# Asking for one ScalarE table set, by name, where exponentials and logarithms alternate

## The chip, the core and the metric

The kernel runs on one core of a Trainium2 chip. The metric is the device time of one execution in microseconds (us). Engines: PE is TensorE's matrix multiply and PEld its weight load, DVE is VectorE, ACT is ScalarE, POOL is GpSimd, SP is SyncE, which here only issues DMAs.

## What is computed

Three transformer blocks are applied to x (1 x 512 x 1024, float32), each once. "norm" is `x * rsqrt(mean(x*x) + 1e-6) * g`.

```python
def first_block(x, p, ...):
    h = rmsnorm(x, norm_mix_g)
    mq, mk, mv, mo, mi, mf, dq, dk, dv, gates = split(h @ w_in)
    ...
    logf = log_sigmoid(f_pre)                        # mLSTM, 4 heads
    hd = diff_attention(...); hd = head_rmsnorm(hd)  # softmax(1) - lam * softmax(2)
    x = x + (sigmoid(g_a) * ya + sigmoid(g_b) * yb) @ w_out
    u = causal_dwconv(rmsnorm(x) @ w_up); val, gt = split(u)
    x = x + (gelu(gt) * val) @ w_down
    x = x + sigmoid(rmsnorm(x) @ w_ple_gate) * (p @ w_ple)
    return rmsnorm(x, norm_final_g)
def second_block(x, ...):                            # two layers
    # stick breaking, 16 heads of 64, blocks of 128 queries
    log_fail = where(mask, log_sigmoid(-z), 0); later = reverse cumsum(log_fail) - log_fail
    a = where(mask, exp(log_sigmoid(z) + later), 0);  x = x + ((a @ v) * silu(gate)) @ w_out
    # latent attention, 8 heads: q, k from ranks 256 and 128, normed per head and rotated
    x = x + (causal_softmax_attention(q, k, v) * silu(gate)) @ w_out
def third_block(x, c, ...):                          # shift, scale, gate = silu(c) @ w_ada + b_ada
    x = x + 0.5 * (1 + gate0) * norm(swiglu(modulate(norm(x))))
    x = x + (1 + gate1) * norm(hybrid_mixer(modulate(norm(x))))   # gated unit + forgetting attention
    x = x + 0.5 * (1 + gate2) * norm(swiglu(modulate(norm(x))))
```

## The kernel before

Every engine runs a list of its own, written out in Python; they meet only at semaphores. Activations are kept feature-major: 8 tiles of 128 features by 512 positions. Weights are used once, in panels of 128 x 2048 float32 (1 MB). A panel goes SP DMA, then an ACT cast to the high half WH (`high`, L1110), then four POOL subtractions for the low half WL (L286), then PE. Each product takes three PE passes: high by high, low by high, high by low (L332, L335, L338; in the stretches where PE multiplies eight fresh feature tiles as they come, L432, L433, L435). Almost all of PE's list is such products. DVE adds results to x, makes low halves and does the attention arithmetic between matmuls.

Two kinds of norm exist. `raw` (L1150) gives PE the tiles scaled by the gain alone, the squares are summed on PE beside the work, and the root is applied to the results. `normalise` (L1184) waits for the root and divides first. In both, ACT makes the root (`root`, L1172) as exp(-0.5 ln(mean + eps)): an ACTIVATE with Ln, a drain, an ACTIVATE with Exp. `post_root` (L1156) is the same for the norm behind each of the third block's sub-layers, `mla_root` (L1641) the same for a head of latent attention. The other users of both functions: the log-sigmoid of the mLSTM gates (from L1250), the roots of differential attention (`da_root`, L1330), the ones of the latents, stick breaking (`ln(1 + exp)`, from L1572, 8 pairs of heads, then exp of the strip sums), the forgetting attention's gates, and the pair of norms behind the gated embedding (`raw_final`, L1517, and the roots behind it).

ACT holds one table set at a time. Nobody asks for one in this kernel: the compiler puts an `ACT_TABLE_LOAD` ahead of an ACTIVATE whose function the set at hand lacks. It takes Exp and Ln from two different sets, so that each change between them is a load; Silu, Sigmoid, Gelu and Sqrt have sets of their own. `ln_ahead` (L1169) is a 128 x 1 Ln, run for nothing but the load that it brings ahead of a `root`.

Of ACT's list for an FFN (`ffn`, L1433): it casts panels, makes the root, applies Gelu or Silu to the gate results, and at its end scales and squares tiles for the next norm. Of a pair of stick breaking: two Exp, two Ln, two casts LBH (L1579), a panel cast, a copy, two Exp of the strips. Of a head of latent attention: copies of transposed blocks (L1683), exps of score blocks with a row sum, projections of the head after next, and after block 0 the root of the next head. What PE waits for in such a head is L898 on it, a product with a diagonal matrix that DVE builds (L2409) from that root.

Of the kernel before, what the change touches and what calls it, by code (L numbers as in the profile page):

```python
# [92 lines left out]
def build(nc, x_in, p_in, par_in, con_in, hot_in, rows_in, sguw_in, w_in, ada_in, rel_tmp, out, stage):  # L93
    with ExitStack() as ctx:
# [1004 lines left out]
        def _(act):  # L1099
# [69 lines left out]
            def ln_ahead():  # L1169
                f(COLS[:, 31:32], par("eps"), ACT.Ln)  # L1170
# [32 lines left out]
            def out_gemm(g0, gain, ahead=False):  # L1203
                for q in range(4):
                    if not (ahead and q == 0):
                        next_panel(g0 + q)
                    if not (ahead and q == 1):
                        skip(2)
                    if q:
                        raw(gain, 2 * q - 2, 2 * q)  # L1210
                ln_ahead()
                raw(gain, 6)
                settle()
# [12 lines left out]

            act.wait_ge(sem("par_dma"), 16)
            ln_ahead()
# [21 lines left out]
            act.dma_start(HOT[0:33, 0:NREL], hot_in).then_inc(sem("hot_dma"), 16)  # L1250
            f(LROW[4][0:4, :], LROW[4][0:4, :], ACT.Exp, scale=-1.0)
# [65 lines left out]
            for half in range(2):  # L1317
                vd_copy(1, half)
            act.wait_ge(sem("lams_ready"), 1)
# [109 lines left out]
            ln_ahead()  # L1429
# [3 lines left out]
            def ffn(g0, conv, shift=None, opened=False):  # L1433
# [33 lines left out]
                root()  # L1467
                if not conv:
                    gate(0)
# [19 lines left out]
                if conv:  # L1489
                    for k in range(DT):  # L1490
                        raw(lambda k: par("norm_ple", k), k, k + 1)
                        if k >= 5:
                            embed(k - 5)
                else:
                    ln_ahead()
                    squares(ACC)
# [29 lines left out]
            for k in range(DT):  # L1526
# [7 lines left out]
                if k:  # L1534
                    raw_final(k - 1)
            raw_final(DT - 1)
# [21 lines left out]
            for q in (2, 3):  # L1558
                gate_panel(G_SBG + q, [SG[:, 2 * q, :], SG[:, 2 * q + 1, :]], ACT.Silu)
            for q in range(4):  # L1560
# [51 lines left out]
            mla_gate(0)  # L1612
            b = take()
# [43 lines left out]

            next_panel(mlh(0))
# [48 lines left out]
            act.dma_start(SGW, sguw_in).then_inc(sem("rows_dma"), 16)  # L1707
            act.wait_ge(sem("fz_ready"), 1)
# [12 lines left out]
            act.drain().then_inc(sem("ug_ready"), 1)  # L1721
            act.wait_ge(sem("lv_ready"), 1)
# [74 lines left out]
            ln_ahead()  # L1797
# [1026 lines left out]
```

## Time and profile before

| | |
|---|---|
| time, median of 3 runs | 2598.78 us (2594.71 to 2599.59) |
| time of the profiled execution | 2599.46 us |
| its span | 2597.6 us (1.9 us lie outside) |
| granted TensorE clock, mean | 0.981 of full speed |
| DMA | 245.50 MB, mean 95 GB/s |
| busy | PE 95%, PEld 76%, DVE 49%, ACT 41%, POOL 39% |
| chain that ended last | PE 62%, issue 15%, DVE 8%, POOL 6%, ACT 5% |
| ... of it, line L1104 of ACT | 3% with a tile, 1% without one |

L1104 is the helper through which nearly every ACTIVATE goes. The loads of table sets carry its line too but have no tile, so the last line's 1% is theirs. Matmul records overlap each other; idle time of PE is read from its waits. PEclk is the granted TensorE clock, of which the records show two levels, 1.2 and 2.4 GHz (0.5 and 1.0).

### The profile page before, as it was taken

To read this page: it belongs to the slowest core of one execution; us is meant where nothing else is said; L and a number is where in the kernel's file an instruction comes from. 1 tells how busy PE (TensorE), PEld (TensorE's weight loads), DVE (VectorE), ACT (ScalarE), POOL (GpSimd) and SP (SyncE) were. 2 spreads that over 40 slices of the span, in tenths; PEclk is the share of its full clock that TensorE was granted. 3 is DMA by queue.
4 is the path that set the end of the run, shared out by engine and by line. 5 is a ranking of instruction groups with operands and counts; after the bars stand their busy time and mean duration, and the time that the engine had idled before them with its cause. 6 is when DMAs were issued, how large, how long until landed. Compare 5 with 4: busy or idle time off the path is not lost.

```text
span 2597.6 us, 31125 instructions
## 1 busy us (share of the span) xinstructions
PE 2457.4 (95%) x11642; PEld 1966.0 (76%) x11642; DVE 1274.6 (49%) x1834; ACT 1062.9 (41%) x1377; POOL 1015.7 (39%) x758
## 2 busy tenths in 40 slices
PE   7999999899999989999988899999999998999999
PEld 5887777788887768777766678888868666788886
DVE  5455567866667661444346562222264444422224
ACT  5435775522222543665546542222253434322222
POOL 3332244444444443212443144444434213344442
PEclk9999999999999999999999999999999999999999
DMA  3221596222222222101221122222212101122221
GB/s 139 77 71 66 194 350 257 106 97 97 97 97 86 78 81 81 49 33 49 97 98 55 44 82 97 97 97 97 97 65 94 57 33 65 51 96 97 96 97 65
DMA packets 35956, 245.50 MB, mean 95 GB/s; under 512 B 3951, under 2 KB 4079, under 8 KB 7188
## 3 DMA queue, kind: packets, MB, share of 16 engines
q1 hardware_dynamic: 30096, 207.12, 22.4%
q10 hardware_dynamic: 5764, 37.06, 3.8%
q8 instruction: 65, 1.06, 0.2%
q14 instruction: 31, 0.25, 0.0%
HBM read 242.06 MB, written 2.11 MB: 94 GB/s over the span
## 4 chain that ended last, share of the span: by engine, by line
PE 62%; issue 15%; DVE 8%; POOL 6%; ACT 5%; DVEq 2%; ACTq 0%; POOLq 0%
PE PS L332 17%; PE PS L338 17%; PE PS L335 16%; POOL WL L286 6%; ACT ARENA L1104 3%; PE PS L432 1%; PE PS L435 1%; PE PS L433 1%; ACT L1104 1%; PE PS L821 1%; DVE LBL L2358 1%; PE PS L1018 1%; PE PS L1030 1%; PE PS L792 1%; PE PS L836 1%
## 5 line engine op out<-in xcount | busy, mean ns | idle before, releaser
L286 POOL TENSOR_TENSOR WL<-WT,WH 128x512 fp32r<-128x512 f32 x754 | 1015.5, 1379 | 1549.3 <-ACT WH L1110 1031.3
L332 PE MATMUL PS<-HH,WH 128*128 128x512 f32 x1568 | 623.2, 397 | 32.0 <-DVE ARENA L1910 7.8
L338 PE MATMUL PS<-HH,WL 128*128 128x512 f32 x1568 | 616.3, 393 | 0.0
L335 PE MATMUL PS<-HL,WH 128*128 128x512 f32 x1568 | 615.6, 393 | 0.0
L1452 ACT CAST WH<-WT 128x2048 fp32r<-128x2048 f32 x90 | 172.1, 1912 | 603.3 <-PE PS L332 603.3
L332 PEld LDWEIGHTS PS<-HH,WH 128*128 128x128 f32 x1568 | 297.8, 190 | 108.6 <-issue 19.5
L338 PEld LDWEIGHTS PS<-HH,WL 128*128 128x128 f32 x1568 | 297.4, 190 | 63.4
L335 PEld LDWEIGHTS PS<-HL,WH 128*128 128x128 f32 x1568 | 297.8, 190 | 60.0 <-issue 0.5
L332 PE MATMUL PS<-YH,WH 128*128 128x512 f32 x840 | 331.2, 394 | 8.0 <-ACT ARENA L1104 3.6
L338 PE MATMUL PS<-YH,WL 128*128 128x512 f32 x840 | 327.3, 390 | 0.0
L335 PE MATMUL PS<-YL,WH 128*128 128x512 f32 x840 | 327.1, 389 | 0.0
L1104 ACT ACTIVATE ARENA<-PS 128x512 f32<-128x512 f32 (+1 forms) x159 | 108.8, 691 | 320.6 <-PE PS L338 220.5
L1110 ACT CAST WH<-WT 128x2048 fp32r<-128x2048 f32 (+1 forms) x99 | 187.6, 1895 | 122.7 <-PE PS L332 100.0
L1104 ACT ACTIVATE ARENA<-ARENA 128x512 f32<-128x512 f32 (+5 forms) x225 | 181.0, 817 | 95.4 <-DVEq L1870 25.5
L2200 DVE TENSOR_TENSOR ARENA<-PS,ARENA 128x512 f32<-128x512 f32 x44 | 30.4, 692 | 376.0 <-PE PS L338 376.0
L332 PEld LDWEIGHTS PS<-YH,WH 128*128 128x128 f32 x840 | 157.7, 188 | 49.3 <-ACT ARENA L1104 5.5
L338 PEld LDWEIGHTS PS<-YH,WL 128*128 128x128 f32 x840 | 157.7, 188 | 33.5 <-POOL WL L286 0.2
L335 PEld LDWEIGHTS PS<-YL,WH 128*128 128x128 f32 x840 | 157.8, 188 | 31.5 <-issue 0.2
L2228 DVE TENSOR_TENSOR ARENA<-PS,ARENA 128x512 f32<-128x512 f32 x176 | 121.3, 691 | 106.3 <-PE PS L338 104.4
L1104 ACT ACT_TABLE_LOAD x103 | 132.1, 1283 | 13.5 <-DVE ARENA L1914 7.2
L432 PE MATMUL PS<-HH,WH 128*128 128x512 f32 x240 | 103.2, 430 | 23.4 <-DVE HL L1841 22.4
L332 PE MATMUL PS<-WH,HH 128*128 128x256 f32 x384 | 111.6, 291 | 7.2 <-DVE HL L1863 5.2
(296 smaller groups left out, 3220.9 us busy)
## 6 DMA issues: line engine op xcount, KB each, us to landing
WT<-weights SPq DMA_DIRECT2D x188, 1024.0 KB, 4.9
ARENA<-w_ada ACTq DMA_DIRECT2D x33, 1024.0 KB, 7.1
ARENA<-w_ada SPq DMA_DIRECT2D x3, 1024.0 KB, 7.6
X<-x_fm SPq DMA_DIRECT2D x4, 512.0 KB, 8.0
out_fm<-X SPq DMA_DIRECT2D x8, 256.0 KB, 2.1
ARENA<-rel_rows ACTq DMA_DIRECT2D x1, 1024.0 KB, 5.3
CON<-constants SPq DMA_DIRECT2D x1, 640.0 KB, 11.5
WT<-weights SPq DMA_DIRECT2D x1, 512.0 KB, 5.0
```

The source lines that it names most:

```text
L286: i = nc.gpsimd.tensor_tensor(WL[s][:, e], WT[s][:, e], WH[s][:, e].bitcast(F32), ALU.subtract)
L332: i0 = nc.tensor.matmul(o, w[0], r[0], start=first, stop=False, skip_group_check=True)
L335: nc.tensor.matmul(o, w[0], r[1], start=False, stop=False, skip_group_check=True)
L338: i2 = nc.tensor.matmul(o, w[1], r[0], start=False, stop=last, skip_group_check=True)
L432: i0 = nc.tensor.matmul(psb(b), w[0], src[0][:, k, :], start=k == 0, stop=False, skip_group_check=True)
L433: i1 = nc.tensor.matmul(psb(b), w[0], src[1][:, k, :], start=False, stop=False, skip_group_check=True)
L435: i2 = nc.tensor.matmul(psb(b), w[1], src[0][:, k, :], start=False, stop=k == DT - 1, skip_group_check=True)
L1104: return nc.scalar.activation(o, i, fn, **kw)
L1110: nc.scalar.copy(WH[s][:, 0:width], WT[s][:, 0:width]).then_inc(sem("w_hi"), 1)
L1452: nc.scalar.copy(WH[s][:, :], WT[s][:, :]).then_inc(sem("w_hi"), 1)
L2200: free(tt(GT[:, q, :], psb(b), GE[:, q, :], ALU.mult), b)
L2228: tt(dst[:, j, :], psb(4 + j % 4), dst[:, j, :], ALU.add).then_inc(sem("b_read"), 1)
```

## The change

All of it is on ACT. `ln_ahead` becomes `ln_exp_table`, which emits one load of the set `natural_log_exp_and_others` by name. It holds both functions. It stands where `ln_ahead` stood and at nine more places in the code, ahead of each stretch that uses Exp and Ln. Inside such a stretch the compiler then adds no load of its own. In `ffn` the set of Gelu or Silu is asked for right behind the root. Nothing is computed differently apart from the tables that Exp and Ln are read from.

```diff
--- before.py
+++ after.py
@@ -1166,8 +1166,8 @@
                     f(SQP[:, k, :], X[:, k, :], ACT.Square).then_inc(sem("sq_ready"), 1)
                 settle(acc=0)
 
-            def ln_ahead():
-                f(COLS[:, 31:32], par("eps"), ACT.Ln)
+            def ln_exp_table():
+                nc.scalar.preload_act_table_set("natural_log_exp_and_others")
 
             def root():
                 act.wait_ge(sem("ms_ready"), n["ms"])
@@ -1208,7 +1208,7 @@
                         skip(2)
                     if q:
                         raw(gain, 2 * q - 2, 2 * q)
-                ln_ahead()
+                ln_exp_table()
                 raw(gain, 6)
                 settle()
 
@@ -1224,8 +1224,8 @@
                     b = take()
                     free(f(dst[q], psb(b), fn), b)
 
+            ln_exp_table()
             act.wait_ge(sem("par_dma"), 16)
-            ln_ahead()
             high(0, 0, PANEL // 2)
             for k in range(DT):
                 if k == 6:
@@ -1248,6 +1248,7 @@
             normalise(last=2, meanwhile=og_last)
             act.wait_ge(sem("az_ready"), 1)
             act.dma_start(HOT[0:33, 0:NREL], hot_in).then_inc(sem("hot_dma"), 16)
+            ln_exp_table()
             f(LROW[4][0:4, :], LROW[4][0:4, :], ACT.Exp, scale=-1.0)
             act.drain()
             f(LROW[4][0:4, :], LROW[4][0:4, :], ACT.Ln, bias=1.0).then_inc(sem("lf_ready"), 1)
@@ -1316,6 +1317,7 @@
             f(MCOL[:, 3, :], MCOL[:, 3, :], ACT.Sqrt, scale=1.0 / P).then_inc(sem("mrs_ready"), 1)
             for half in range(2):
                 vd_copy(1, half)
+            ln_exp_table()
             act.wait_ge(sem("lams_ready"), 1)
             f(COLS[:, 25:27], COLS[:, 25:27], ACT.Exp).then_inc(sem("lame_ready"), 1)
 
@@ -1426,7 +1428,7 @@
                     for k in (2 * q - 2, 2 * q - 1):
                         raw(lambda k: par("norm_ffn", k), k, k + 1, YH)
                         ada_sums(2)
-            ln_ahead()
+            ln_exp_table()
             raw(lambda k: par("norm_ffn", k), 6, DT, YH)
             settle()
 
@@ -1465,6 +1467,7 @@
                 if not opened:
                     high(g0 + 1, (g0 + 1) % 2)
                 root()
+                nc.scalar.preload_act_table(ACT.Gelu_apprx_tanh if conv else ACT.Silu)
                 if not conv:
                     gate(0)
                 if conv:
@@ -1487,12 +1490,13 @@
                 next_panel(g0 + 3 * CH - 1)
                 tiles[0] = t0 + 4 * CH
                 if conv:
+                    ln_exp_table()
                     for k in range(DT):
                         raw(lambda k: par("norm_ple", k), k, k + 1)
                         if k >= 5:
                             embed(k - 5)
                 else:
-                    ln_ahead()
+                    ln_exp_table()
                     squares(ACC)
                 settle(DT - 1 if conv else POST_ACC)
                 n["ge"] = e0 + 2 * CH
@@ -1533,6 +1537,7 @@
                 act.drain().then_inc(sem("pg_ready"), 1)
                 if k:
                     raw_final(k - 1)
+            ln_exp_table()
             raw_final(DT - 1)
             settle()
 
@@ -1557,6 +1562,7 @@
             sb_gate(3)
             for q in (2, 3):
                 gate_panel(G_SBG + q, [SG[:, 2 * q, :], SG[:, 2 * q + 1, :]], ACT.Silu)
+            ln_exp_table()
             for q in range(4):
                 v_panel(G_SBV + q, SV, 256 * q)
             qk_copy(G_SBQK, SQ_, SK_, 0, "sqk_ready", scale=SB_D ** -0.5)
@@ -1610,6 +1616,7 @@
                     free(f(LG[:, 2 * q + e, :], psb(b), ACT.Silu), b)
 
             mla_gate(0)
+            ln_exp_table()
             b = take()
             free(f(RQ, psb(b), ACT.Ln, scale=1.0 / Q_RANK, bias=par("eps")), b)
             b = take()
@@ -1655,6 +1662,7 @@
                 f(PB[:, v % 2, 0:P * (j + 1)], PS[:, 2 + v % 2, 0:P * (j + 1)], ACT.Exp, scale=COLS[:, c:c + 1],
                   bias=COLS[:, 16 + j:17 + j], accum_out=COLS[:, j:j + 1]).then_inc(sem("pe_exp"), 1)
 
+            ln_exp_table()
             next_panel(mlh(0))
             mla_proj(0)
             next_panel(G_MLV)
@@ -1705,6 +1713,7 @@
             act.dma_start(LNB, rows_in[:, 0:1024].rearrange("p (k n) -> p k n", k=2)).then_inc(sem("rows_dma"), 16)
             act.dma_start(SGB, rows_in[:, 1024:1536].rearrange("p (q i) -> p q i", q=4)).then_inc(sem("rows_dma"), 16)
             act.dma_start(SGW, sguw_in).then_inc(sem("rows_dma"), 16)
+            ln_exp_table()
             act.wait_ge(sem("fz_ready"), 1)
             f(NCUM[0:8, :], NCUM[0:8, :], ACT.Exp, scale=-1.0)
             act.drain()
@@ -1719,6 +1728,7 @@
             act.drain().then_inc(sem("vg_ready"), 1)
             gate_panel(G_U[1], [UG[:, 2, :], UG[:, 3, :]], ACT.Gelu_apprx_tanh)
             act.drain().then_inc(sem("ug_ready"), 1)
+            ln_exp_table()
             act.wait_ge(sem("lv_ready"), 1)
             f(STAT[:, 40:44], STAT[:, 40:44], ACT.Ln, bias=par("eps"))
             act.drain()
@@ -1794,7 +1804,7 @@
                     skip(2)
                 if q:
                     squares(ACC, 2 * q - 2, 2 * q)
-            ln_ahead()
+            ln_exp_table()
             squares(ACC, 6)
             settle(POST_ACC)
             post_root()
```

ACT's list has 103 loads before and 41 after. The other engines' lists are the same in both kernels.

**Stick breaking**, ACT, one pair of heads, before (LBH are the casts that L821 of PE takes):

```order
L1104 ACTIVATE ARENA<-ARENA 128x1280 x2
L1104 ACT_TABLE_LOAD
L1104 ACTIVATE ARENA<-ARENA 128x1280 x2
L1579 CAST LBH<-ARENA 128x1280 x2
L1110 CAST WH<-WT 128x2048
L1104 ACTIVATE ARENA<-PS 128x512
L1104 ACT_TABLE_LOAD
L1104 ACTIVATE ARENA<-PS 128x1280 x2
L1591 COPY ARENA<-PS 128x512
L1104 ACTIVATE ARENA<-PS 128x1280
L1104 ACTIVATE ARENA<-ARENA 128x1280 x2
```

and now (L1579 and L1591 have become L1585 and L1597):

```order
L1104 ACTIVATE ARENA<-ARENA 128x1280 x4
L1585 CAST LBH<-ARENA 128x1280 x2
L1110 CAST WH<-WT 128x2048
L1104 ACTIVATE ARENA<-PS 128x512
L1104 ACTIVATE ARENA<-PS 128x1280 x2
L1597 COPY ARENA<-PS 128x512
L1104 ACTIVATE ARENA<-PS 128x1280
L1104 ACTIVATE ARENA<-ARENA 128x1280 x4
```

Both loads of the pair are gone: the one between Exp and Ln, and the one between Ln and the Exp of the strips.

**The norms behind the gated embedding**, ACT, from the last `raw_final` to the first copies of the normalised x, before (YH, scaled by COLS, is the last tile that PE needs):

```order
L1104 ACTIVATE YH<-X,COLS 128x512
L1104 ACTIVATE ARENA<-X 128x512
L1104 ACTIVATE ARENA<-X,PAR 128x512
L1110 CAST WH<-WT 128x2048
L1104 ACT_TABLE_LOAD
L1104 ACTIVATE ARENA<-ARENA,PAR 128x512
L1104 ACT_TABLE_LOAD
L1104 ACTIVATE ARENA<-ARENA 128x512
L1104 ACT_TABLE_LOAD
L1104 ACTIVATE ARENA<-PS,PAR 128x512
L1104 ACT_TABLE_LOAD
L1104 ACTIVATE ARENA<-ARENA 128x512
L1104 ACT_TABLE_LOAD
L1104 ACTIVATE ARENA<-PS 128x512 x2
L1110 CAST WH<-WT 128x2048
```

and now:

```order
L1170 ACT_TABLE_LOAD
L1104 ACTIVATE YH<-X,COLS 128x512
L1104 ACTIVATE ARENA<-X 128x512
L1104 ACTIVATE ARENA<-X,PAR 128x512
L1110 CAST WH<-WT 128x2048
L1104 ACTIVATE ARENA<-ARENA,PAR 128x512
L1104 ACTIVATE ARENA<-ARENA 128x512
L1104 ACTIVATE ARENA<-PS,PAR 128x512
L1104 ACTIVATE ARENA<-ARENA 128x512
L1104 ACT_TABLE_LOAD
L1104 ACTIVATE ARENA<-PS 128x512 x2
```

The two roots have no load between them or ahead of them; the load by name stands ahead of the last tile.

**The start of latent attention**, ACT, from the last Silu of the gates to the first head's root, before:

```order
L1104 ACTIVATE ARENA<-PS 128x512 x2
L1110 CAST WH<-WT 128x2048
L1104 ACTIVATE ARENA<-PS 128x512
L1104 ACTIVATE ARENA<-PS,PAR 128x512
L1104 ACTIVATE ARENA<-PS 128x512
L1104 ACTIVATE ARENA<-PS,PAR 128x512
L1104 ACTIVATE ARENA<-PS 128x512
L1110 CAST WH<-WT 128x2048
L1628 COPY ARENA<-PS 128x512 x4
L1104 ACT_TABLE_LOAD
L1104 ACTIVATE COLS<-PS,PAR 128x8
L1104 ACT_TABLE_LOAD
L1104 ACTIVATE COLS<-COLS 128x8
```

and now:

```order
L1104 ACTIVATE ARENA<-PS 128x512 x2
L1170 ACT_TABLE_LOAD
L1110 CAST WH<-WT 128x2048
L1104 ACTIVATE ARENA<-PS 128x512
L1104 ACTIVATE ARENA<-PS,PAR 128x512
L1104 ACTIVATE ARENA<-PS 128x512
L1104 ACTIVATE ARENA<-PS,PAR 128x512
L1104 ACTIVATE ARENA<-PS 128x512
L1110 CAST WH<-WT 128x2048
L1635 COPY ARENA<-PS 128x512 x4
L1104 ACTIVATE COLS<-PS,PAR 128x8
L1104 ACTIVATE COLS<-COLS 128x8
```

The load by name stands ahead of the cast of the first panel, and both loads at the head's root are gone. The same two loads go in the other seven heads.

## Rows read from the trace of the kernel before

**Rows 1.** Page, busy time of each engine: us, share of the span, instructions.

```profile
PE 2457.4 (95%) x11642; PEld 1966.0 (76%) x11642; DVE 1274.6 (49%) x1834; ACT 1062.9 (41%) x1377; POOL 1015.7 (39%) x758
```

**Rows 2.** Page, costliest groups: busy us, mean ns, idle us before it and releaser.

```profile
L1104 ACT ACT_TABLE_LOAD x103 | 132.1, 1283 | 13.5 <-DVE ARENA L1914 7.2
```

**Rows 3.** Waits of PE: waiting line, releaser; us in total, times, longest us.

```profile
PE PS L432 <- DVE HL L1841: 22.4, 9, 10.5
PE PS L332 <- DVE HL L1863: 11.8, 14, 1.7
...
PE PS L821 <- ACT LBH L1579: 7.8, 8, 1.3
PE PS L332 <- ACT ARENA L1104: 7.7, 5, 2.2
PE PS L898 <- DVE ARENA L2409: 7.5, 6, 1.6
PE PS L821 <- DVE LBL L2358: 5.5, 16, 0.9
...
PE PS L836 <- ACT ARENA L1104: 2.1, 7, 0.3
...
PE PS L1086 <- DVE ARENA L2505: 0.9, 1, 0.9
```

**Rows 4.** Timeline of ACT, end of the gate: start us, us, instruction, [idle <-releaser].

```profile
921.24 0.73 ACT L1104 ACTIVATE ARENA<-ARENA,PAR 128x512 f32<-128x512 f32 x1 [4.19 <-DVEq L2312]
922.03 1.28 ACT L1104 ACT_TABLE_LOAD   x1
923.32 0.63 ACT L1104 ACTIVATE ARENA<-ARENA 128x512 f32<-128x512 f32 x1
...
927.96 1.28 ACT L1104 ACT_TABLE_LOAD   x1
```

**Rows 5.** Timeline of PE, first matmul behind that gate.

```profile
929.99 0.77 PE L432 MATMUL PS<-YH,WH 128*128 128x512 f32 x1 [3.50 <-ACT ARENA L1104]
```

**Rows 6.** Windows, just behind it: us, busy of PE, PEld, DVE, ACT, POOL, PEclk.

```profile
929.80:933.40 3.60, 3.41 (x9) 2.73 (x10) 0.10 (x1) 3.08 (x5) 0.57 (x1) 0.54 0.01 2
```

**Rows 7.** Timeline of ACT, then PE, one stick-breaking pair.

```profile
1081.07 1.28 ACT L1104 ACT_TABLE_LOAD   x1
...
1086.57 0.68 PE L821 MATMUL PS<-LBH,CONR 128*128 128x512 f32 x2 [1.01 <-ACT LBH L1579]
```

**Rows 8.** Timeline of ACT, DVE and PE, one latent-attention head.

```profile
1393.31 1.28 ACT L1104 ACT_TABLE_LOAD   x1
...
1392.83 0.43 DVE L2441 CAST YH<-ARENA 128x512 fp32r<-128x512 f32 x1
1394.87 0.69 DVE L2409 TENSOR_TENSOR ARENA<-CON,COLS 128x512 f32<-128x512 f32 x1 [1.62 <-ACTq L1647]
...
1395.71 0.46 PE L898 MATMUL PS<-ARENA,CON 128*128 128x128 f32 x2 [1.55 <-DVE ARENA L2409]
```

**Rows 9.** Timeline of ACT and DVE, a norm behind a sub-layer (post_root).

```profile
1907.81 1.28 ACT L1104 ACT_TABLE_LOAD   x1
...
1909.74 0.75 DVE L2492 SCALAR_TENSOR_TENSOR ARENA<-ARENA,MOD,PS 128x512 f32<-128x512 f32 x1 [5.03 <-ACT PS L1104]
```

**Rows 10.** Timeline of PE, two places where ACT holds it up in blocks one and two.

```profile
58.51 0.35 PE L332 MATMUL PS<-WH,HH 128*128 128x256 f32 x1 [1.92 <-ACT ARENA L1104]
...
290.34 0.47 PE L332 MATMUL PS<-HH,WH 128*128 128x512 f32 x1 [2.19 <-ACT ARENA L1104]
```

**Rows 11.** Timeline of PE, end of the first FFN, then start of latent attention.

```profile
848.84 0.50 PE L332 MATMUL PS<-YH,WH 128*128 128x512 f32 x1 [1.60 <-ACT ARENA L1505]
...
1329.64 0.50 PE L332 MATMUL PS<-YH,WH 128*128 128x512 f32 x1 [1.90 <-ACT ARENA L1104]
...
1340.44 0.50 PE L332 MATMUL PS<-WH,YH 128*128 128x512 f32 x1 [1.11 <-ACT ARENA L1628]
```

**Rows 12.** Page, DMA issues: times, KB each, median us from issue to landing.

```profile
CON<-constants SPq DMA_DIRECT2D x1, 640.0 KB, 11.5
```

## The prediction

> **What bounds the kernel.** I begin with the busy shares. PE is at 95% [rows 1]: of the span of 2597.6 us only about 134 us are idle, so no change to another engine can bring more, and it brings something only where PE waits for that engine. ACT is busy 41% of the time. The costliest groups give the matter of this change its size: 103 table loads, 132.1 us, 1283 ns each [rows 2]. 62 of them go (103 against 41 in the lists), which is 62 x 1.283 = 79.5 us of ACT. Most lie beside PE work. The question is which stand ahead of a wait of PE.
>
> The waits of PE answer it [rows 3]. Only four rows name ACT as releaser and have loads ahead of them: L821 behind the casts LBH (7.8 us, 8 times), L836 (2.1, 7 times), L332 behind L1104 (7.7, 5 times), and one wait of 3.50 at the gated embedding [rows 5]. In four others DVE is the releaser, but DVE itself waits for ACT's root: L898 behind L2409 (7.5, 6 times), two of the waits for L1841, some of those behind L1863, and L1086. A row says how long PE waits, not how much a load caused; each place has to be walked through in the timeline.
>
> **What one load is worth.** At the gated embedding Ln runs from 921.24 for 0.73, its end is 921.97, and Exp starts at 923.32 [rows 4]: a change of set takes 1.35 end to end, the load 1.28 of it, and a drain that the code asks for anyway the rest. I take 1.28 to 1.30 per load on a path.
> The Trainium skill, "ScalarE: Activation LUTs", section "What ACT_TABLE_LOAD costs", gives the same load and about 1380 ns of drain besides, 2.66 us for each change of set. The load agrees with the trace, the total does not (1.35). By the page every load on a path would bring twice as much, and the sum below would be about 61 us in place of 31; the row decides, and the idle time of PE at most of these places would not hold it either.
>
> **The sum, in order of size** (us saved).
> 1. *Stick breaking, eight pairs: 12.1.* In each pair the load between Exp and Ln, the one at 1081.07 [rows 7], is on the way to the casts LBH, and PE's L821 stands 1.01 behind them. It needs the first cast 1.28 earlier, so the 1.01 closes. The load ahead of the strips' Exp opens L836's gap of 0.3. All of L821's wait for ACT (7.8) and all of L836's (2.1) go [rows 3]. L821 also waits for DVE's LBL, twice a pair, 5.5 in 16 waits [rows 3]; the first of each two is fed by the same Ln and goes, the second is DVE's own and stays. The first is the shorter one, so I take 2.2 of the 5.5. 7.8 + 2.1 + 2.2 = 12.1. Next late is PE itself, whose products fill the rest of the pair, so nothing more is to be had here.
> 2. *Heads of latent attention: 7.5.* The two loads of a head's root go, of which the second starts at 1393.31. DVE's L2409 waits 1.62 for that root, PE's L898 1.55 for L2409 [rows 8]. Without the loads the root is there before DVE ends L2441 at 1393.26; L2409 starts then and not at 1394.87, 1.6 earlier. That covers the gap, six times: the whole row of 7.5 [rows 3]. DVE's own list is late next, with nothing to spare.
> 3. *The norms behind the gated embedding: 3.3.* Three of the four loads from 922.03 to 927.96 [rows 4] go; that behind them (Sigmoid or Silu) stays. ACT's results come 3 x 1.29 = 3.9 earlier, PE's wait is 3.50 [rows 5] and closes. The load by name, which is now ahead of the last tile for PE, delays it a little: 0.2 of its 1.28, since ACT is 4.19 idle behind it [rows 4]. 3.5 - 0.2 = 3.3.
> 4. *Norms behind sub-layers, two inner ones: 2.5, and the last: 0.9.* The load at 1907.81 stands between Ln and Exp; DVE's L2492 waits 5.03 for it [rows 9] and the next norm's tiles, for which PE waits at L1841 (its row holds 22.4 in nine waits, so there is room) [rows 3], hang on that chain. 2 x 1.26. At the end of the program only 0.9 of the same load shows as PE's wait at L1086 [rows 3], which I take.
> 5. *Block one: 2.8.* At the mLSTM gates one of three loads goes, under a PE wait of 1.92: 1.3. At the last root of differential attention PE waits 2.19 [rows 10]; one load goes, and DVE's division ahead of it is not far off on its own: 1.5, for this load and what its earlier roots gave.
> 6. *The roots of the second and third FFN: 1.2 each.* PE takes DVE's tiles (L1863) as they come behind the root, with 11.8 of waits in 14 [rows 3], about 3 of them at each of these two roots: the whole train moves by a load.
> 7. *Costs.* A load by name ahead of the tail of the first FFN delays what PE waits for at 848.84 by 1.60 [rows 11]. The DVE chain beside it sets the pace, so I take 0.6, between 0 and 1.28. At the start of latent attention the load stands ahead of a cast, and the wait of 1.90 at 1329.64 grows by 1.28; the one of 1.11 at 1340.44 [rows 11] goes, for L1628's copies are behind two loads less. Net 0.2. The other loads by name stand where ACT waits anyway, for DVE or PE: nothing. If that cover were gone, 1.28 each.
> The loads elsewhere (first root, first FFN's root, the latents' roots, the forgetting attention's gates) have other work ending last at their place: nothing.
>
> 12.1 + 7.5 + 3.3 + 2.5 + 0.9 + 2.8 + 2.4 - 0.6 - 0.2 = 30.7 us. Besides, behind PE's wait at 929.99 the granted clock is 0.54 over 3.6 us [rows 6], the lower of the two levels nearly all the time: a stretch at half speed costs about 1.8. It follows an idle stretch of PE of 3.50, and this one closes. With it 32.5. From the profiled execution of 2599.46 that is 2567.0; the median of the runs shown is 0.7 below that execution, so against it 2566.3. I forecast **2566.0 us**.
>
> **Bounds.** Lower saving: places 4 to 6 (8.6) are paths through DVE, which may be at its own pace as at the first FFN; if half of each load is lost there, -4.3; the costs at their full 1.28 each, -1.8; a new half-speed stretch or two, -3.6. That gives 32.5 - 4.3 - 1.8 - 3.6 = 22.8, thus 2576. Upper: the costs at nothing (+0.8), and the rival of the clock below.
>
> **Rivals.**
> *R1: hidden anyway.* ACT is 41% busy and PE 95% [rows 1], so 62 loads could all be slack. For it: only a slice of the waits names ACT. Against it: the sum's two largest terms are whole rows of waits with the load directly ahead. It would give 2598.8. Chance 0.04.
> *R2: the clock comes back too.* At about 18 places PE runs some 3.5 us at half clock, several right behind a wait that closes or shrinks: four of them are behind places 2, 5 and 6. If these go full speed as well, 1.8 each, 7.2 to 9 more: 2557 to 2559. Against: stretches at half clock also stand where PE had hardly waited, so closing one gap may only move them. Chance 0.15.
> *R3: a set asked for by name is no table at hand but is fetched each time* (slower). All 103 loads of the trace are the compiler's and take 1283 ns on the mean; none shows the combined set. About five loads by name are ahead of something PE waits for: 58.51, 848.84 and 1329.64 [rows 10, 11], the gated embedding [rows 5] and the latents. If each took T more, the loss is 5 T against 32.5: it decides from T = 6.5 us. The nearest fetch by DMA is 11.5 us to landing, for the constants [rows 12]; 5 x 11.5 = 57.5 gives 2623.5. Against it: six sets are in use before and none takes longer than another; the combined one replaces two of them, so no more are in use. Chance 0.03.
> The same page says that all sets are placed at model start, and refilled by DMA only in a program with more than eight. By it R3 is out, and no run here has shown more than six.
> *R4: partly lost.* DVE or the paces of PE's in-order list absorb places 2 and 4 to 6 altogether, about half of the sum: some 17 us remain, 2581.5. Chance 0.10.
> *R5: the compiler puts its own loads back.* The lists show 41, so this is excluded, but for loads which the chip treats otherwise; no chance of its own.
>
> **How the numbers follow.** Forecast 0.68, R1 0.04, R2 0.15, R3 0.03, R4 0.10. The range 2554 to 2577 holds the forecast with its bounds and R2. Beyond 0.2% (5.2 us, about what a measurement of this kernel can tell from no change): faster 0.93 (forecast, R2, R4), slower 0.03 (R3), the same 0.04 (R1).
>
> **What would show it.** Right: 41 loads of 1283 ns; L821's wait for LBH, L836's for ACT and L898's for L2409 gone; a pair of stick breaking about 1.5 shorter; the wait at the gated embedding below 0.5; mean of a load by name equal to the others'. Wrong: loads at L1170 longer than 1283 ns (R3); the same waits under another releaser, DVE's L2358 or L2441 (R4); waits of PE at L332 behind the cast at the start of latent attention over 3.5. The granted clock would rise above 0.981 by R2, and stay otherwise.

## The result, and the profile after

| | before | changed |
|---|---|---|
| median | 2599.11 us (2594.71 to 2599.59, 4 runs) | 2576.88 us (2572.69 to 2579.92, 4 runs) |
| profiled execution | 2599.46 us | 2579.63 us |
| its span | 2597.6 us | 2577.5 us |
| granted clock, mean | 0.981 | 0.978 |

The ratio is 0.9917 (95% interval 0.9897 to 0.9938): the change saves 0.8%, 21.6 us of 2599 (16 to 27 by the interval). What is called saved here and below is worked out from such a ratio; the medians alone differ by up to 2.6 us from it. The forecast was 2566.0, 33 us saved, in a range up to 2577. The median, 2576.88, lies on that end of the range, 11 us above the forecast, and by the ratio the time is 2577.5. Of what had been put into the sum, a third is missing.

Now the profile of the changed kernel. First the busy times, as in [rows 1]:

```profile
PE 2463.6 (96%) x11642; PEld 1974.0 (77%) x11642; DVE 1268.2 (49%) x1834; ACT 984.3 (38%) x1308; POOL 1012.5 (39%) x758
```

ACT is busy 78.6 us less, as 62 loads of 1.283 promise (79.5). PE is busy 6.2 us *more*, with the same 11642 matmuls. That is the first sign: PE did not get other work, it ran part of it slower. Its idle time, summed over all its waits, fell from 135.0 to 108.3 us, by 26.7, and the span by only 20.1.

The loads, grouped by line (columns as in [rows 2]; L1170 is the set by name, L1470 the one behind an FFN's root):

```profile
L1104 ACT ACT_TABLE_LOAD x22 | 28.2, 1283 | 1.2 <-DVE PS L1844 0.8
L1170 ACT ACT_TABLE_LOAD x16 | 20.5, 1283 | 8.3 <-DVE ARENA L1924 7.2 <-PEq L2827 0.7
L1470 ACT ACT_TABLE_LOAD x3 | 3.8, 1283 | 0.1
```

41 loads, and a set asked for by name costs the same 1283 ns as any other. R3 is out.

The waits of PE, to be held against [rows 3]:

```profile
PE PS L432 <- DVE HL L1851: 20.7, 11, 10.4
PE PS L332 <- DVE HL L1873: 10.3, 12, 1.7
...
PE PS L332 <- ACT ARENA L1104: 8.5, 7, 3.3
...
PE PS L821 <- DVE LBL L2368: 4.7, 15, 0.5
PE PS L332 <- issue: 4.6, 3, 2.7
```

L821's wait for LBH (7.8), L836's for ACT (2.1), L898's for the root (7.5) and L1086's (0.9) are gone altogether. So most of the waits went where the forecast had them go. What came back is in the clock. The 200 us from 1300 to 1500 hold the heads of latent attention in both kernels, though the changed one is some 14 us further on in its list there (columns: window, us, busy of PE, PEld, DVE, ACT, POOL, granted clock, DMA share, GB/s). First before:

```profile
1300.00:1500.00 200.00, 172.52 (x890) 134.13 (x889) 109.08 (x220) 107.65 (x193) 66.49 (x51) 0.95 0.19 64
```

and the changed kernel:

```profile
1300.00:1500.00 200.00, 180.27 (x885) 141.22 (x884) 102.39 (x212) 90.27 (x181) 61.99 (x48) 0.90 0.19 67
```

A granted clock of 0.95 over 200 us, of levels 1.0 and 0.5, is 2 x 0.05 x 200 = 20 us at half clock; 0.90 is 40. PE is busy 7.7 us more with 5 matmuls fewer. One head of the changed kernel shows it in single rows of PE, where [rows 8] had the wait of 1.55:

```profile
1379.09 1.92 PE L890 MATMUL PS<-CON,ARENA 128*128 128x1 f32 x16 [0.65 <-DVE ARENA L2413]
1380.87 1.19 PE L911 MATMUL PS<-ARENA 128*128 128x384 f32 x2
1381.85 1.49 PE L912 MATMUL PS<-ARENA 128*128 128x384 f32 x2
1382.57 0.88 PE L913 MATMUL PS<-CONR 128*128 128x128 f32 x1
1383.24 0.63 PE L950 MATMUL PS<-CON,ARENA 128*128 128x128 f32 x2
1383.67 0.64 PE L922 MATMUL PS<-ARENA 128*128 128x128 f32 x2
1384.09 1.37 PE L898 MATMUL PS<-ARENA,CON 128*128 128x128 f32 x8
```

The same head before the change:

```profile
1390.34 1.92 PE L890 MATMUL PS<-CON,ARENA 128*128 128x1 f32 x16 [0.66 <-DVE ARENA L2403]
1392.12 0.89 PE L911 MATMUL PS<-ARENA 128*128 128x384 f32 x2
1392.85 0.81 PE L912 MATMUL PS<-ARENA 128*128 128x384 f32 x2
1393.19 0.52 PE L913 MATMUL PS<-CONR 128*128 128x128 f32 x1
1393.55 0.39 PE L950 MATMUL PS<-CON,ARENA 128*128 128x128 f32 x2
1393.77 0.39 PE L922 MATMUL PS<-ARENA 128*128 128x128 f32 x2
```

L898 waits no longer. But from the start of L911 to the start of L898 the changed kernel takes 1384.09 - 1380.87 = 3.22 us; before it took 1395.71 - 1392.12 = 3.59 with the whole wait of 1.55 in it. The granted clock tells why (same columns as above):

```profile
1377.20:1381.00 3.80, 3.13 (x26) 2.97 (x27) 2.92 (x7) 0.81 (x3) 0.00 (x0) 1.00 0.67 237
1381.00:1384.60 3.60, 3.60 (x13) 2.56 (x13) 3.04 (x7) 0.71 (x3) 0.00 (x0) 0.55 0.12 46
```

It falls to the lower level just behind the sixteen one-column products of L890, after 0.65 of waiting. Before, in this head, it did not:

```profile
1388.40:1394.20 5.80, 5.04 (x34) 4.16 (x34) 3.88 (x9) 3.25 (x6) 0.00 (x0) 1.00 0.53 184
```

### The profile page after: what moved, and what is told of

It is laid out like the page before. It is cut to its first block, busy times and chain, and to the rows that moved or that the text cites. A ratio compares the mean times of both kernels' runs of the same rounds, so it can differ in the third digit from the quotient of the medians.

```text
span 2577.5 us, 31057 instructions
## 1 busy us (share of the span) xinstructions
PE 2463.6 (96%) x11642; PEld 1974.0 (77%) x11642; DVE 1268.2 (49%) x1834; ACT 984.3 (38%) x1308; POOL 1012.5 (39%) x758
## 4 chain that ended last, share of the span: by engine, by line
PE 66%; issue 15%; DVE 8%; POOL 6%; ACT 3%; DVEq 2%; POOLq 0%; ACTq 0%
PE PS L332 17%; PE PS L338 17%; PE PS L335 17%; POOL WL L286 6%; ACT ARENA L1104 2%; PE PS L432 2%; PE PS L433 1%; PE PS L435 1%; PE PS L821 1%; DVE LBL L2368 1%; PE PS L1018 1%; PE PS L1030 1%; PE PS L792 1%; PE PS L836 1%; PE PS L890 1%
## 5 line engine op out<-in xcount | busy, mean ns | idle before, releaser
L332 PE MATMUL PS<-HH,WH 128*128 128x512 f32 x1568 | 624.4, 398 | 30.9 <-DVE ARENA L1920 7.8
L332 PEld LDWEIGHTS PS<-HH,WH 128*128 128x128 f32 x1568 | 298.2, 190 | 108.0 <-issue 18.7
L332 PE MATMUL PS<-YH,WH 128*128 128x512 f32 x840 | 331.6, 395 | 10.1 <-ACT ARENA L1104 6.3
L332 PEld LDWEIGHTS PS<-YH,WH 128*128 128x128 f32 x840 | 157.9, 188 | 50.9 <-ACT ARENA L1104 8.9
L432 PE MATMUL PS<-HH,WH 128*128 128x512 f32 x240 | 102.6, 427 | 21.7 <-DVE HL L1851 20.7
L332 PE MATMUL PS<-WH,HH 128*128 128x256 f32 x384 | 111.2, 290 | 6.2 <-DVE HL L1873 4.7
L1104 ACT ACTIVATE ARENA<-PS,COLS 128x128 f32<-128x128 f32 (+3 forms) x102 | 57.4, 564 | 156.1 <-DVE COLS L2596 59.4
```

Source lines behind the costliest of these rows:

```text
L332: i0 = nc.tensor.matmul(o, w[0], r[0], start=first, stop=False, skip_group_check=True)
L432: i0 = nc.tensor.matmul(psb(b), w[0], src[0][:, k, :], start=k == 0, stop=False, skip_group_check=True)
L1104: return nc.scalar.activation(o, i, fn, **kw)
```

## The experiments

Two theories stood against each other. *Clock*: the work saved is nearly what was forecast, and about 7 us come back through time at half clock, in these two traces 2 x (1 - 0.978) x 2577.5 = 113 us against 2 x (1 - 0.981) x 2597.6 = 99. *Paths*: the terms of the sum are too large, since a gap that closes opens another. A third, *luck*: the half-clock stretches differ between executions and mean nothing.

### The change once more, and its two largest parts alone

**Again**: the changed kernel, nothing edited.

> The changed kernel itself, once more. Clock theory (the work saved is near the forecast's 31 us, and some 8 us of it come back as more time of PE at the lower clock, 113 us against 97 by the two traces): about 2577 against 2599, and the trace again with over 110 us at half clock, the most of it in the heads of latent attention. Luck theory (which stretches run at half clock differs from one execution to the next, and the trace at hand was an unlucky one): a trace with 100 us or less at half clock and a time of 2570 or below. Paths theory (the work saved is only 22 us): the half-clock time varies and the time does not follow it.

**Stick breaking alone**, onto the kernel before:

```diff
                 gate_panel(G_SBG + q, [SG[:, 2 * q, :], SG[:, 2 * q + 1, :]], ACT.Silu)
+            ln_exp_table()
             for q in range(4):
                 v_panel(G_SBV + q, SV, 256 * q)
```

> Before, with the set by name ahead of stick breaking alone. By the forecast's term of 12.1 and nothing from the root behind it: 2587. Clock theory: the same, 12 us, since in both traces PE never falls to half clock in the pairs (PE 200 us long at 1.00). Paths theory: less than 9.

**Latent attention alone**, onto the kernel before:

```diff
+            ln_exp_table()
             next_panel(mlh(0))
             mla_proj(0)
```

> Before, with the set by name ahead of latent attention alone, where the change has it. The forecast's terms are 7.5 for the heads, 1.2 for the root of the second FFN behind them, less 0.2 at the start: 8.5 faster, 2590.6. Clock theory: the waits at L898 are gone, but each head now has a stretch at half clock, some 1.7 us each and six of them more than before; the time is within 3 us of before. Paths theory (the gap returns at another wait in the head): the same time, but by waits of PE and not by the clock.

**Latent attention undone**, in the changed kernel: this one line out.

```diff
-            ln_exp_table()
             next_panel(mlh(0))
             mla_proj(0)
```

> The change with the set by name ahead of latent attention taken out again, so that each head has its two loads. By the forecast 7.3 slower than the change: 2584. Clock theory: the waits of L898 are back at 1.55 and the half-clock stretches are down to about two heads in six, so it is within 2 us of the change, 2575 to 2579. Paths theory: the same as the clock theory in time, but with the half-clock time unchanged.

Measured on one chip, before at 2598.74 (17 runs). "Half clock" is worked out, as above, from the granted clock of the window 1300 to 1500 of each run's one trace, in steps of 4 us:

| | median us | ratio (95%) | saved us | half clock |
|---|---|---|---|---|
| again | 2572.83 | 0.9909 (0.9894 to 0.9924) | 23.6 | 44 |
| stick breaking alone | 2583.98 | 0.9947 (0.9933 to 0.9960) | 13.8 | 28 |
| latent attention alone | 2598.18 | 0.9996 (0.9985 to 1.0007) | 1.0 | 40 |
| latent attention undone | 2575.24 | 0.9915 (0.9901 to 0.9930) | 22.1 | 28 |

Stick breaking alone brings 13.8 (10.4 to 17.4); the forecast had 12.1. The two kernels have the same 11642 matmuls in the same order, so a lead can be read: how much earlier the same matmul starts in the changed kernel. Across the pairs it grows from 1.7 to 14.6 us, by 12.9. That term holds. The set by name ahead of latent attention brings nothing that can be measured, alone (1.0, between -1.8 and 3.9) or as part of the change: with it 0.9909 and 0.9917, without it 0.9915, intervals that lie almost on one another. Yet the wait that it was to remove is gone wherever it is in, and back where it is out, as in this row of the waits of PE of the kernel with latent attention undone:

```profile
PE PS L898 <- DVE ARENA L2418: 5.6, 5, 1.6
```

With the loads in the heads, three traces (before, stick breaking alone, undone) show 20, 28 and 28 us at half clock; without them, three traces (changed, again, alone) show 40, 44 and 40. So in the heads it is not luck: it goes with the loads. Over a whole execution it can't be seen. The mean granted clock of all executions on this chip is 0.979 for the kernel before (17, from 0.975 to 0.982) and 0.979 for the changed one (6), and the 99 against 113 us above owe part of their difference to the traces at hand.

How much it costs is read head by head, from the start of L890 in one head to its start in the next. Of the seven such lengths in a trace the first two are left out, because PE waits 3.57 at L950 in the first and a stretch at half clock begins in or behind that wait; five are left. First two neighbours of the kernel with latent attention undone, so with the loads:

```profile
1371.66:1389.48 17.82, 16.79 (x89) 12.96 (x89) 11.23 (x26) 11.57 (x22) 5.16 (x4) 0.90 0.17 63
1389.48:1407.30 17.82, 15.27 (x89) 11.96 (x89) 11.23 (x26) 11.57 (x22) 5.17 (x4) 1.00 0.16 57
```

and one of the changed kernel:

```profile
1396.80:1414.50 17.70, 16.69 (x90) 12.88 (x90) 11.32 (x26) 9.00 (x20) 5.16 (x4) 0.90 0.18 62
```

A short stretch at half clock costs a head with the loads 0 to 0.3 us (17.8 to 18.1): PE arrives later at L898, and its wait there of 1.55 is gone or smaller. In a head without the loads there is no such wait to hide it. Longer stretches (0.82 to 0.83 over a head) bring the head to 19.3 to 19.9 us with or without the loads. In the four traces without loads and without further products (changed, again, alone, and the late load below) each of the twenty heads has a stretch, and none takes less than 17.7 us; with the loads nine heads of fifteen have one. So all but a tenth of a us of a head's saving is used up: 17.8 with the loads and full clock, 17.7 without them and with the shortest stretch.

The paths theory asked for other waits and an unchanged clock; neither is there. The expectation for "again" said about 2577 for the clock theory and it came out at 2572.8; the ratio, 0.9909 against 0.9917, is the same within the intervals.

### The load ahead of the first cast

**Late**, in the changed kernel: the load moves behind the first value products, directly ahead of the first head's root.

```diff
-            ln_exp_table()
             next_panel(mlh(0))
             mla_proj(0)
             next_panel(G_MLV)
             mla_v(0, 2)
+            ln_exp_table()
             mla_root(0)
```

> The change, with the load by name at the start of latent attention moved from ahead of the first cast to directly ahead of the first head's root, where ACT idles 1.34 for PE anyway. The forecast had charged 0.2 for its place. If the load ahead of the cast costs its full length (the wait at L332 grew from 1.90 to 3.32), this is 1.3 faster than the change, about 2571.5 beside the 2572.8 of the same chip, and the wait is back at 1.9. If its place costs nothing, no difference.

2573.60 us, ratio 0.9913 (0.9897 to 0.9928). The trace does what was said: PE's wait for this cast, 3.32 in the changed kernel, is 1.90 again, as before the change. First the changed kernel:

```profile
1316.50 0.79 PE L332 MATMUL PS<-YH,WH 128*128 128x512 f32 x1 [3.32 <-ACT ARENA L1104]
```

then with the load late:

```profile
1308.58 0.66 PE L332 MATMUL PS<-YH,WH 128*128 128x512 f32 x1 [1.90 <-ACT ARENA L1104]
```

The measured times can't tell 1.4 us apart: inconclusive there, clear in the trace.

### Holding the clock

The kernel has a helper, `keep_warm`, that repeats a 128x512 product into a bank whose content is overwritten afterwards. **Three products per head** in the wait ahead of L890, in the changed kernel:

```diff
             def mla_sums(h):
                 b = take()
+                keep_warm(psb(b), 3 if h else 0)
                 pe.wait_ge(sem("hc_ready"), h + 1)
```

> The change, with three more 512-column products (results overwritten) on PE in every head from the second on, in its 0.65 us wait ahead of the sums of squares. Clock theory: PE falls to half clock there because it does next to nothing from that wait to the end of the sixteen one-column products; with the three products most of the seven heads' stretches go, 40 us at half clock in latent attention become 20 or less, and 7 or more us are saved: about 2566. If the falls come from something else than PE's own work, no fewer stretches, and the same time or 1 us more.

**Five per head**: besides these, two ahead of L898.

```diff
             def mla_spread(h):
                 b = take()
+                keep_warm(psb(b), 2 if h else 0)
                 pe.wait_ge(sem("hdiag_ready"), h + 1)
```

> As the last, and two more products ahead of L898, where PE waits no longer, so that they cost 0.45 us a head in six heads, 2.7 us. Clock theory: a gain over the last only if stretches are left there; otherwise 2.7 slower than it, about 2569. Otherwise: 3 to 4 slower than the change.

**The loads back, three products**: latent attention undone, with the first of these edits.

> The two loads of every head back, and the three products ahead of the sums. Clock theory: the half-clock time in latent attention falls below the 27 us that it has with the loads, but the waits of 1.55 at L898 stay, so it is slower than the version with the products and without the loads by up to the 7.5 of the forecast's term: about 2571 to 2573. That would be the term, seen with the clock held.

**Latent attention alone, five products**: onto the kernel before.

> Before, with the set by name ahead of latent attention alone, and the three and two more products per head. Clock theory: what the set by name saves there shows once the clock is held: 7.5 for the heads, 1.2 for the next root, less 1.4 for the load ahead of the cast and up to 2.7 for the products that no wait covers: 5 to 8 faster than before. Without the clock's part in it, the version without the products was level with before, and this one would be level or up to 3 slower.

The first three ran on one chip with the late load (before at 2595.51, 9 runs), the last in a later job (before at 2595.01, 17 runs):

| | median us | ratio (95%) | saved us | half clock |
|---|---|---|---|---|
| load late, no products | 2573.60 | 0.9913 (0.9897 to 0.9928) | 22.6 | 40 |
| changed, three products | 2566.14 | 0.9877 (0.9862 to 0.9892) | 31.9 | 24 |
| changed, five products | 2564.18 | 0.9875 (0.9860 to 0.9890) | 32.4 | 20 |
| loads back, three products | 2574.40 | 0.9911 (0.9898 to 0.9925) | 23.1 | 16 |
| latent attention alone, five | 2588.62 | 0.9971 (0.9959 to 0.9982) | 7.5 | 12 |

This settles it. The same products that save 9 us without the loads (22.6, with the load late, to 31.9) save nothing measurable with them (22.1 to 23.1, on two chips). With the clock held, leaving the loads out is worth 31.9 - 23.1 = 8.8 us, on one chip, give or take about 5 by the intervals. The two traces say it without that noise. Between the first L890 and the last, seven heads, the kernel with products takes 127.8 us with the loads and 118.2 without them, 9.6 less, both with 10 us at half clock, all of it at the opening; without products the same stretch takes 129.5 (undone) against 127.5 (changed) and 128.5 (again). One head of each with products, first with the loads, then without:

```profile
1408.49:1426.32 17.83, 15.85 (x93) 12.37 (x92) 11.23 (x26) 11.57 (x22) 5.17 (x4) 1.00 0.18 62
```

```profile
1407.15:1423.27 16.12, 15.76 (x93) 12.37 (x92) 11.16 (x26) 8.99 (x20) 5.17 (x4) 1.00 0.19 67
```

With the loads a head takes 17.83 with the products and 17.82 without them, so what they do at the clock is hidden behind L898's wait. That is the forecast's term, 1.7 a head, there all the time and paid back in clock. Latent attention alone with five products saves 7.5 (4.7 to 10.6) where it had saved nothing. That it is just the 7.5 of the forecast is chance: the root of the second FFN, the load ahead of the first cast and what the products cost and save at the opening are in it too, and the kernel before with these products and nothing else was not run. Its window, where without products it had 0.90:

```profile
1300.00:1500.00 200.00, 184.14 (x961) 144.90 (x960) 110.71 (x224) 92.71 (x183) 69.86 (x54) 0.97 0.19 69
```

The two further products ahead of L898 were expected to cost 2.7 or to pay by stretches left there; five against three is 0.5 by the ratios, not to be told apart in the times. In the traces they cost 0.3 a head (16.45 against 16.12) and remove no stretch that the three had left there.

### A faster version

**Late load, five products, longer rows ahead of two norms**: `WARM`, the count of such products ahead of the first tile of a norm, goes from 8 to 20. The expectation speaks of three norms; the trace has such rows of products at two, at 1882 and 2163 us.

```diff
-WARM = 8
+WARM = 20
```

> The change with the load of latent attention moved late, three and two products per head, and the row of products that the kernel already runs ahead of three norms lengthened from 8 to 20, into the 3.23 us for which PE still waits there. Clock theory: 2 to 3 stretches fewer behind those waits, 1.7 each, and 1.4 for the load: 4 to 6 faster than the version with the five products, about 2559. If those stretches come from PE's waits behind the first tile, 1 to 2 faster only.

**More**: that, and products in two further waits.

```diff
                 if second:
+                    keep_warm(psb(2), 30)
                     pe.wait_ge(sem("sq_acc2"), DT - 1)
...
+                if not v:
+                    keep_warm(PS[:, 4, :], 12)
                 pe.wait_ge(sem("pn_ready"), v + 1)
```

> The last, with 30 products in the wait of 8.5 at the gated embedding's second norm and 12 in the wait of 3.5 ahead of the first head's transposes. Clock theory: two or three stretches fewer again, 3 to 5 faster than the last. If the stretch begins inside the wait and not because of it, no difference.

The first is a miss: 2564.23 us, ratio 0.9876 (0.9855 to 0.9898), where 2559 was expected, no better than without. The waits ahead of the first tiles were filled, and the stretches at half clock behind them are gone at both norms, yet no time is. The first norm, from the start of its first tile (L432) to the start of its second, with 8 products (the changed kernel with five products a head) and then with 20:

```profile
1884.42:1887.80 3.38, 2.98 (x6) 1.17 (x6) 3.16 (x3) 1.24 (x2) 2.77 (x2) 0.57 0.00 0
```

```profile
1887.53:1890.89 3.36, 1.84 (x5) 0.86 (x5) 3.16 (x3) 1.25 (x2) 2.76 (x2) 1.00 0.00 0
```

The tiles come from DVE, which is busy 3.16 us in both, and PE at full clock only waits longer for the second one: 0.39 became 1.53. Here, where another engine sets the pace, the stretch at half clock had cost nothing.

The second took 2557.30 us, ratio 0.9851 (0.9827 to 0.9876), 7 us less, with a mean clock of 0.991 over its span of 2554.1. It is the fastest of all: 38.7 us under the kernel before and some 16 under the change (38.7 less the 21.6 to 23.6 of its two measurements). By the traces the two waits share the gain: the heads, first L890 to last, take 115.7 us where they took 120.1, with no time at half clock left in them, and from the start of the wait at the gated embedding to the next wait at L332 it is 28.4 where it was 31.1. Which of the two edits a single us belongs to was not measured apart. In every other trace a stretch at half clock begins inside that wait of 8.57 at the gated embedding; in this one none does.

## Why the prediction was wrong

Most of the waits that it read went as it said, but a wait that goes is not yet time saved, and at two places it was not. The leads show where the time came and went, in us gained over the kernel before in each stretch (times of the kernel before; one trace each). The forecasts are the sum's terms with their costs, by place. The last column has the loads of before in all stretches but the third, and so shows what differs between executions:

| stretch | forecast | changed | again | undone | sticks alone |
|---|---|---|---|---|---|
| 0 to 850, block one up to its FFN's end | 2.2 | 1.4 | 9.0 | 7.0 | -1.6 |
| 850 to 1025, gated embedding | 5.1 with the clock | 0.3 | 1.9 | 1.6 | 0.2 |
| 1025 to 1310, stick breaking | 12.1 | 12.9 | 12.9 | 12.9 | 13.0 |
| 1310 to 1560, latent attention, second FFN's root | 8.5 | -0.9 | -0.6 | -0.4 | 1.0 |
| 1560 to 2000, first norm behind a sub-layer | 1.3 | 1.8 | 0.7 | 0.6 | 0.0 |
| 2000 to 2190, forgetting attention | 0 | 1.4 | 1.4 | 1.4 | 0.0 |
| 2190 to the end, second norm, third FFN's root, last norm | 3.3 | 3.6 | 3.0 | 2.9 | 1.2 |
| sum | 32.5 | 20.5 | 28.3 | 26.0 | 13.8 |

Of the 12 us that the trace of the changed kernel lacks, 9.4 are missing in latent attention and 4.8 at the gated embedding. "Undone" has the loads back in the heads and loses nothing by it there. The forgetting attention's 1.4 was not forecast. Block one moves by several us from trace to trace, with one and the same kernel.

1. *Stick breaking*, forecast 12.1: 12.9 in the trace, 13.8 measured alone. Its parts were not all right: L821's waits for LBL fell by 0.8 and not by the 2.2 that the sum took, and all waits of PE in the pairs together by 10.6 (15.4 to 4.8); where the other 2.3 come from is not shown, so that the term comes out within a us is in part luck. The first cast LBH is ready and PE has no wait ahead of it, the second load is gone too:

```profile
1053.75 1.26 ACT L1104 ACTIVATE ARENA<-ARENA 128x1280 f32<-128x1280 f32 x1
1055.47 1.27 ACT L1585 CAST LBH<-ARENA 128x1280 fp32r<-128x1280 f32 x1 [0.46 <-DVE ARENA L2361]
...
1056.84 1.56 PE L821 MATMUL PS<-LBH,CONR 128*128 128x512 f32 x10
1058.66 1.61 PE L821 MATMUL PS<-LBL,CONR 128*128 128x512 f32 x10 [0.26 <-DVE LBL L2368]
```

2. *Heads of latent attention*, forecast 7.5: **the step that failed.** It took the whole row of waits at L898 for saved, and the clock as unchanged in a head whose wait is gone. The wait went, DVE's L2419 started early as forecast, and each of the twenty heads had a stretch at half clock, with nothing left to hide it: 17.7 us a head where it was 17.8, and 16.1 only once products held the clock.

```profile
1381.58 0.43 DVE L2451 CAST YH<-ARENA 128x512 fp32r<-128x512 f32 x1
1381.92 0.69 DVE L2419 TENSOR_TENSOR ARENA<-CON,COLS 128x512 f32<-128x512 f32 x1
```

3. *Gated embedding*, forecast 3.3. The three loads are gone and so is PE's wait of 3.50 [rows 5]:

```profile
920.02 0.72 ACT L1104 ACTIVATE ARENA<-ARENA,PAR 128x512 f32<-128x512 f32 x1 [4.48 <-DVEq L2322]
920.81 0.63 ACT L1104 ACTIVATE ARENA<-ARENA 128x512 f32<-128x512 f32 x1
...
922.75 1.28 ACT L1104 ACT_TABLE_LOAD   x1
```

But a wait of 0.56 at the next panel, which the forecast had not named, becomes 2.70. Its row names no releaser; in both kernels PE starts 0.73 behind the end of DVE's L1834 (now L1844), so PE meets DVE sooner. From 925 us to that panel the lead still grows by 3.1; a stretch at half clock behind the new wait then takes 1.6 of it, and over the whole stretch from 850 to 1025 it is 0.3 here and 1.6 to 1.9 in the other traces of the table.

```profile
939.87 0.47 PE L332 MATMUL PS<-HH,WH 128*128 128x512 f32 x1 [2.70 <-issue]
```

4. *Norms behind sub-layers*, forecast 2.5 and 0.9: the waits of 4.50 and 4.49 are 3.22 each, 2.6 in all, and L1086's 0.9 is gone.

```profile
1900.17 0.79 PE L432 MATMUL PS<-HH,WH 128*128 128x512 f32 x1 [3.22 <-DVE HL L1851]
```

5. *Block one*, forecast 2.8: the wait of 2.19 became 0.70, 1.5 as taken, and that of 1.92 became 1.44, 0.5 where 1.3 was taken. The lead grows by more than that, by 4.0 to 4.6 from 260 to 300 us. What is gained there then passes the merge of the branches, where DVE waits for the tiles of `w_ada` and PE for DVE; those waits differ by a few us between traces of the same kernel, so this term can't be read to the microsecond. Up to 850 us the lead is 1.4, 9.0 and 7.0 in three traces with the loads gone.
6. *Roots of the FFNs*, forecast 2.4: L1873's waits fell from 11.8 to 10.3, 1.5. The second FFN's root brought 0.4 of it in the lead, the third's about 1.
7. *Costs*, forecast 0.6 and 0.2. At the end of the first FFN nothing (the wait of 1.60 is the same). At latent attention the wait grew by 1.42 to 3.32 and the 1.11 went, 0.3 by the waits and as forecast. In the lead the opening, from 1310 to 1356, costs 1.6 and with the late load nothing (0.3 gained), so it was avoidable.

Outside the heads the forecast had 32.5 - 7.5 - 1.8 for the clock = 23.2. The change without its part in the heads measures 22.1 (18.2 to 25.7). So outside the heads the sum came out, with errors in both directions that about cancel, and it was wrong in one term and in the sign of the clock. The clock had been priced as a gain: 1.8 behind the gated embedding in the forecast, up to 9 in R2. Only the lower bound held the other sign, "a new half-speed stretch or two", 3.6, and it was tied to no place; in the heads alone seven stretches stand in the trace where three had stood. In fact the stretch behind the gate's first wait went and another stood 10 us later, so the 1.8 was not gained. Of the rivals, R4 came nearest in size (2581.5) for a reason that wasn't the right one; R1, R2, R3 and R5 did not happen.

The price per load was right. Ln ends at 920.74 and Exp starts at 920.81, 0.07 later with no load between, drain included; with the load it was 1.35 [rows 4]. A change of set therefore costs 1.28 here, the load alone. The 1380 ns of drain that the Trainium skill adds to it ("ScalarE: Activation LUTs", section "What ACT_TABLE_LOAD costs") are not in these rows. What the same page of the Trainium skill says in "Table sets: the hidden batching unit", that `natural_log_exp_and_others` holds both functions and one load does, holds: no load stands between these two.

**What stays open**: why heads with a 1.55 us wait of PE keep the higher clock more often (six of fifteen) than heads without (none of twenty). In these heads the fall comes 0.9 to 2.8 us behind the start of L890, where PE has waited 0.65 and then runs sixteen products of one column; with three 128x512 products in that wait no such head has a stretch, in either kernel. Why idle time a little later helps as well was not explained. It is also not shown what three products alone would do to the kernel before.

## What to carry to other kernels

Walk a saving of ScalarE down to a wait of PE and price it by that wait: 79.5 us of loads were worth 22, and the reading of waits named most of the places in advance. Then ask of each stretch that gets denser what PE's weakest moment in it is: a wait that closes can be paid for in clock, and the time will look as if nothing had happened. Where the wait is gone and the time is not, compare the granted clock and the length of the same piece of work in both traces, and fill the weak moment with a few products that nobody reads. Do it where PE sets the pace; where DVE did, at the norms, the clock rose from 0.57 to 1.00 and the time stayed.

## What was not expected of the hardware

PE at half clock goes with *less* waiting here: 40, 44, 40 and 40 us in latent attention without the loads against 20, 28 and 28 with them. A stretch at half clock is free where PE would wait anyway: 17.82 us for a head at a mean clock of 0.90 and 17.82 for its neighbour at 1.00, both with the wait; without it 17.70 and 16.12. Three 128x512 products per head, 0.7 us of work inside a wait of 0.65, brought 40 us at half clock down to 24 and saved 9 us. Loads of a set take 1283 ns whether the compiler places them or the kernel names the set.
